# A last FFN on unnormalized tiles, a final norm on transposed tiles, and three weight borders moved by 64 bytes

## The chip, the core and the metric

The kernel runs on one core of a Trainium2 chip. The metric is the device time of one execution in microseconds (us). TensorE (PE) multiplies, VectorE (DVE), ScalarE (ACT) and GpSimd (POOL) do the work on tiles, SyncE (SP) issues every DMA. The page and the trace come from one profiled execution; "span" is the time from its first to its last instruction.

## The reference, cut to what matters

The input is one sequence of 256 tokens with 1024 features. Two hybrid attention layers run first and then a second block of two layers with shift, scale and gate vectors that depend on a condition. Each layer of the second block is a half FFN, a mixer (Fourier, then retention), and another half FFN. The diff touches the last FFN and the final norm most.

```python
def half_ffn(t, m, j):
    h = modulate(rmsnorm_2(t, norm_g[l, j]), m[3 * j], m[3 * j + 1])      # h * (1 + scale) + shift
    return t + 0.5 * m[3 * j + 2] * swiglu(h, ffn_w_gate[l, j // 2], ffn_w_up[l, j // 2], ffn_w_down[l, j // 2])
...
x = x + m_lat[5] * y_lat          # end of the retention mixer
x = half_ffn(x, m_lat, 2)         # the last FFN, on the 256 tokens of x only
return rmsnorm_2(x, final_g)
```

`rmsnorm_2` divides by the root of the mean square over the 1024 features of a token; `swiglu` is silu(h @ w_gate) * (h @ w_up), 2816 wide, times w_down.

## The kernel before, in words

**Layout.** Activations lie transposed: 128 features on the partitions, tokens along the free axis, so x is 8 tiles (`KT`) of 128 x 256 (`T`). A weight matrix arrives in chunks of 128 x 1024 float32, one output tile per chunk. Every product is made of three matmuls in float32r, on a high and a low part of both operands: `w_high` x `h_high`, `w_high` x `h_low`, `w_low` x `h_high` (lines 1861 to 1863 in `products`, 1873 to 1875 in `one`, 2357 to 2359 in `ro`). One chunk is thus 24 matmuls.

**Weight ring.** Chunks go round in a ring of 4 slots. SP loads `raw`, ACT copies it to `w_high` (`split`, line 565), POOL subtracts to get `w_low` (line 1021), three chunks ahead of TensorE (`AHEAD`). `W8` puts the split weights at an offset of 64 bytes in the slot (`LINE` = 16 floats), `WIDE` at 0. Chunks used with 256 columns mostly take the first form and chunks used with 512 columns (x and context together) the second, but the first three chunks of `up0`, `up1` and `up2` are `WIDE` although their matmuls have 256 columns each: they run twice, once for each half (`chunk_trio`), while the norm before them is still being finished.

**Order.** Each engine runs a list written out by hand, with counting semaphores between them. The stages near the end are `rg` and the retention heads, `ro` (16 chunks, two for each tile of x), a norm, `up3` (44 chunks: gate and up tiles in turns), `down3` (32 chunks, four for each tile of x), the final norm and one store.

**The norm before `up3`.** During `ro` DVE adds each output tile to x (line 1814), squares it (1173) and adds the squares (1176). After the last tile TensorE sums over the partitions with a matmul on a matrix of ones (1836), ACT takes the root (612), DVE the reciprocal (1154); then tile by tile DVE multiplies by gain and 1/root (1162), ACT adds the shift (621) and copies the high part (625), POOL makes the low part (1050). TensorE waits for tile after tile (`tile_ready`).

**`up3`.** For each pair of chunks ACT takes SiLU of the gate bank (865), DVE multiplies it with the up bank (1572) and casts the product to its high part (1575), POOL makes the low part (`act_low`, 1111). The PSUM banks of a pair are used again two pairs later.

**The end.** In `down3` DVE adds and squares each tile (1600, 1173, 1176). Then the same norm without a shift: sum, root, reciprocal, eight multiplications on DVE and eight copies on ACT (634), and one store of 1 MB (551) in feature order; the host transposes the result.

Of the kernel before, what the change touches and what calls it, by code (L numbers as in the profile page):

```python
# [164 lines left out]
def program(nc, xT_d, cols_d, cond_d, ada_d, w1_d, wv_d, wu_d, wd_d, w2_d, rope_d, mask_d, ident_d, identb_d,  # L165
            dft_d, rope2_d, dist_d, out_d):
    with ExitStack() as ctx:
# [39 lines left out]
        rs = keep("rs", [P, 2 * T])  # L207
        sT = at("sT", [P, 4, T], F32, top[0])
# [6 lines left out]
        top8 = keep("top8", [P, 8])  # L215
        late = top[0] + (x_at - top[0]) % 256
# [145 lines left out]
        own_std = sem("own_std")  # L362
        stored = sem("stored")
        passed = sem("passed")
# [73 lines left out]
        def _(e):  # L438
# [111 lines left out]
            e.wait_ge(normed, 4 + 3 * KT)  # L550
            e.dma_start(out_d.rearrange("(k p) t -> p k t", p=P), hf[:, :, 0:T]).then_inc(stored, 16)
            e.wait_ge(stored, 16)
# [3 lines left out]
        def _(e):  # L556
# [51 lines left out]

            def norm(cols_n, shift, dest, has_split):

                e.wait_ge(sq_summed, n_sq())
                e.activation(rs[:, 0:cols_n], ps[:, 7, 0:cols_n], ACT.Sqrt, bias=eps[:, :], scale=1.0 / D)\
                    .then_inc(std_done, 1)
                if has_split and shift:
                    with turns(e, KT // 4, (n_scaled, 4), (n_shifted, 4)) as i:
                        for pair in ((0, 1), (2, 3)):
                            for j in pair:
                                e.wait_ge(scaled, n_scaled())
                                for q in range(cols_n // T):
                                    part = nb[:, j, T * q:T * q + T]  # L620
                                    last = e.activation(part, part, ACT.Identity, bias=shift(4 * i + j, q))
                                last.then_inc(shifted, 1)
                            for j in pair:
                                e.wait_ge(shifted, n_shifted())
                                e.activation(flat(hh, 4 * i + j, 0, cols_n), nb[:, j, 0:cols_n], ACT.Copy)\
                                    .then_inc(norm_hi, 1)
                    return
                with turns(e, KT // 4, (n_scaled, 4)) as i:
                    for j in range(4):
                        e.wait_ge(scaled, n_scaled())  # L630
                        for q in range(cols_n // T):
                            src, out = nb[:, j, T * q:T * q + T], dest(4 * i + j, q)
                            if shift is None:
                                last = e.activation(out, src, ACT.Copy)
                            else:
                                last = e.activation(out, src, ACT.Identity, bias=shift(4 * i + j, q))
                        last.then_inc(norm_hi if has_split else normed, 1)
# [208 lines left out]
            stepped(laps("out"), W8, WIDE, 0, OUT, None, context_and_squares)  # L846
# [10 lines left out]
            def up(f, halves, all_split=None):  # L857
                base = later[f"up{f}"]

                def silu(i, j):  # L860
# [4 lines left out]
                    e.activation(tn[:, j // 2, 0:halves * T], ps[:, j - 1, 0:halves * T], ACT.Silu)\  # L865
                        .then_inc(act_step, 1)

                if f < ADA_FFNS:
                    e.wait_ge(cond_in, 16 * LAYERS + 32 * f + 32)
                    e.wait_ge(norm_split, all_split)  # L870
                    for q in range(2):
                        e.activation(cond_bank(q), ada2[q][:, :], ACT.Silu).then_inc(c_silu, 1)
# [274 lines left out]
        def _(e):  # L1147
# [674 lines left out]
            with turns(e, KT // 2, (step, 4)) as i:  # L1822
                for j in range(2):
                    add_tile(3, 5, 2 * i + j, j, 1)
# [690 lines left out]
```

## Time and profile before

| | us |
|---|---|
| runs (3) | 2327.92, 2334.66, 2335.64; median 2334.66 |
| the profiled execution, its own time | 2331.55 |
| its span | 2329.8 |
| PE busy in the span | 2269.9 |
| POOL busy | 1352.6 |
| DVE busy | 1105.4 |
| ACT busy | 843.7 |

A timeline row reads: start, duration, engine, line, operation, output and inputs, shape, count; in brackets the idle time of the engine before it and what ended it. The duration of a matmul is its passage through the pipeline, so neighbours overlap; the distance between two starts is what one costs in a stream. In the windows view PEclk is the granted TensorE clock, 1.00 for 2.4 GHz and 0.50 for 1.2 GHz.

### The profile page before, as it was taken

What the parts mean: (1) busy time and instruction counts of PE and PEld (TensorE: products, weight loads), DVE (VectorE), ACT (ScalarE), POOL (GpSimd) and SP (SyncE); (2) the same over time, 40 slices, a digit from 0 to 9 for tenths busy, and PEclk for the clock granted to TensorE, in tenths of its full rate; (3) what the DMA queues carried; (4) which work ended last, traced back from release to release, by engine and by line L of the source; (5) the groups of instructions that cost most, each with busy time, mean ns of one, the idle gap of its engine ahead of it and who ended that gap; (6) DMA issues with size and microseconds to landing.
All of it is one profiled execution on the core that took longest, in us unless ns stands there. A gap on an engine that the chain in (4) does not pass through costs nothing.

```text
span 2329.8 us, 39284 instructions
## 1 busy us (share of the span) xinstructions
PE 2269.9 (97%) x13534; PEld 1997.9 (86%) x13534; DVE 1105.4 (47%) x2078; ACT 843.7 (36%) x1250; POOL 1352.6 (58%) x712
## 2 busy tenths in 40 slices
PE   8999999999999999999999999999999999998997
PEld 7988999888888888868888888888888988998997
DVE  6753468543765543267555422655522520245223
ACT  5454453544522212213322222422222423655653
POOL 6864788647665554403555443555544544468996
PEclk9999999999999999999999999999999999998998
DMA  8842468523365543301655433455533422224554
GB/s 290 272 145 73 136 230 290 185 80 124 121 226 198 197 143 100 115 31 55 226 180 201 158 93 98 172 202 194 190 92 96 167 91 100 97 98 150 188 180 135
DMA packets 112846, 356.58 MB, mean 153 GB/s; under 512 B 13168, under 2 KB 22896, under 8 KB 112368
## 3 DMA queue, kind: packets, MB, share of 16 engines
q1 hardware_dynamic: 112752, 355.31, 46.1%
q8 instruction: 61, 1.00, 0.2%
q14 instruction: 33, 0.27, 0.0%
HBM read 347.66 MB, written 1.05 MB: 150 GB/s over the span
## 4 chain that ended last, share of the span: by engine, by line
PE 82%; POOL 6%; DVE 4%; issue 4%; ACT 1%; DMA 1%; DVEq 0%; SPq 0%; POOLq 0%; ACTq 0%
PE ps L1861 22%; PE ps L1862 22%; PE ps L1863 22%; POOL w_low L1021 5%; PE ps L1992 2%; PE ps L2010 1%; PE ps L1912 1%; PE ps L1911 1%; PE ps L1910 1%; PE ps L2223 1%; PE ps L2319 1%; PE ps L2213 1%; DMA raw<-in_w_dram 1%; PE ps L2000 1%; DVE ps L1288 1%
## 5 line engine op out<-in xcount | busy, mean ns | idle before, releaser
L1021 POOL TENSOR_TENSOR w_low<-raw,w_high 128x1024 fp32r<-128x1024 f32 (+3 forms) x542 | 1204.5, 2232 | 685.5 <-ACT w_high L565 684.7
L565 ACT ACTIVATE w_high<-raw 128x1024 fp32r<-128x1024 f32 (+3 forms) x544 | 537.6, 990 | 1142.4 <-PE ps L1863 902.1
L1861 PE MATMUL ps<-h_high,w_high 128*128 128x256 f32 (+1 forms) x2720 | 892.4, 328 | 22.5 <-POOL h_low L1050 6.4
L1862 PE MATMUL ps<-h_low,w_high 128*128 128x256 f32 (+1 forms) x2720 | 882.3, 324 | 0.0
L1863 PE MATMUL ps<-h_high,w_low 128*128 128x256 f32 (+1 forms) x2720 | 882.1, 324 | 0.0
L1861 PEld LDWEIGHTS ps<-h_high,w_high 128*128 128x128 f32 x2720 | 515.7, 190 | 70.5 <-issue 9.2
L1863 PEld LDWEIGHTS ps<-h_high,w_low 128*128 128x128 f32 x2720 | 516.3, 190 | 42.8
L1862 PEld LDWEIGHTS ps<-h_low,w_high 128*128 128x128 f32 x2720 | 515.7, 190 | 42.6
L1861 PE MATMUL ps<-act_high,w_high 128*128 128x512 f32 (+1 forms) x770 | 266.2, 346 | 0.0
L1862 PE MATMUL ps<-act_low,w_high 128*128 128x512 f32 (+1 forms) x770 | 265.6, 345 | 0.0
L1863 PE MATMUL ps<-act_high,w_low 128*128 128x512 f32 (+1 forms) x770 | 265.6, 345 | 0.0
L1572 DVE TENSOR_TENSOR hn<-tn,ps 128x512 f32<-128x512 f32 (+1 forms) x88 | 54.7, 621 | 382.9 <-PE ps L1863 318.3
L1111 POOL TENSOR_TENSOR act_low<-hn,act_high 128x512 f32 (+3 forms) x88 | 102.0, 1159 | 210.6 <-DVE act_high L1575 210.6
L1862 PEld LDWEIGHTS ps<-act_low,w_high 128*128 128x128 f32 x770 | 145.1, 188 | 18.2
L1863 PEld LDWEIGHTS ps<-act_high,w_low 128*128 128x128 f32 x770 | 145.1, 188 | 18.1
L1861 PEld LDWEIGHTS ps<-act_high,w_high 128*128 128x128 f32 x770 | 145.1, 188 | 18.0
L1247 DVE SCALAR_TENSOR_TENSOR sq<-ada,ps 128x1024 f32<-128x1024 f32 x120 | 146.5, 1221 | 17.2
L1243 DVE SCALAR_TENSOR_TENSOR sq<-ada,ps 128x1024 f32<-128x1024 f32 x120 | 146.1, 1218 | 8.9 <-DMA ada<-in_ada_dram 0.3
L1600 DVE SCALAR_TENSOR_TENSOR x<-ps,gate,x 128x256 f32 (+1 forms) x50 | 22.3, 481 | 262.6 <-PE ps L1863 262.2
L1873 PE MATMUL ps<-h_high,w_high 128*128 128x256 f32 x248 | 75.6, 305 | 14.6 <-DVE h_low L1186 8.2
L1910 PE MATMUL ps<-w_high,h_high 128*128 128x512 f32 (+1 forms) x224 | 83.6, 373 | 1.6 <-POOL w_low L1021 1.6
L1912 PE MATMUL ps<-w_high,h_low 128*128 128x512 f32 (+1 forms) x224 | 83.3, 372 | 0.0
(213 smaller groups left out, 2332.0 us busy)
## 6 DMA issues: line engine op xcount, KB each, us to landing
raw<-in_w_dram SPq DMA_DIRECT2D x216, 512.0 KB, 3.5
raw<-in_wu_dram SPq DMA_DIRECT2D x176, 512.0 KB, 4.5
ada<-in_ada_dram SPq DMA_DIRECT2D x144, 512.0 KB, 4.0
raw<-in_wd_dram SPq DMA_DIRECT2D x64, 384.0 KB, 3.1
raw<-in_wd_dram SPq DMA_DIRECT2D x64, 320.0 KB, 2.9
raw<-in_wv_dram SPq DMA_DIRECT2D x24, 408.0 KB, 4.8
heads<-rot SPq DMA_DIRECT2D x96, 64.0 KB, 3.6
ada<-in_cond_dram SPq DMA_DIRECT2D x6, 512.0 KB, 5.0
```

The lines of the kernel that those rows point to most:

```text
L565: e.activation(wh[:, c % RING, at_:at_ + w], raw[:, c % RING, 0:w], ACT.Copy).then_inc(hi_done, 1)
L1021: e.tensor_tensor(wl[:, c % RING, at_:at_ + w], raw[:, c % RING, 0:w], wh[:, c % RING, at_:at_ + w].bitcast(F32), ALU.subtract).then_inc(l ...
L1111: e.tensor_tensor(flat(al, 2 * i + j // 2, 0, halves * T), hn[:, j // 2, 0:halves * T], flat(ah, 2 * i + j // 2, 0, halves * T).bitcast(F3 ...
L1243: e.scalar_tensor_tensor(out=trash, in0=ada2[half][:, :], scalar=1.0, in1=cond_bank(0), op0=ALU.mult, op1=ALU.mult, accum_out=mod[:, bass. ...
L1247: e.scalar_tensor_tensor(out=trash, in0=ada2[half][:, :], scalar=1.0, in1=cond_bank(1), op0=ALU.mult, op1=ALU.mult, accum_out=mod[:, bass. ...
L1572: e.tensor_tensor(hn[:, j, 0:w], tn[:, j, 0:w], ps[:, 2 * j + 1, 0:w], ALU.mult)\
L1861: e.matmul(ps[:, bank, to:to + n], wh[:, j, w], hi, start=(first and t == tiles[0]), stop=False)
L1862: e.matmul(ps[:, bank, to:to + n], wh[:, j, w], low, start=False, stop=False)
L1863: end = e.matmul(ps[:, bank, to:to + n], wl[:, j, w], hi, start=False, stop=(last and t == tiles[-1]))
L1873: e.matmul(out, wh[:, j, w], hi, start=first, stop=False)
L1910: e.matmul(out, hh[:, k, tok], wh[:, j, w], start=(first and t == 0), stop=False)
L1912: end = e.matmul(out, hl[:, k, tok], wh[:, j, w], start=False, stop=(last and t == 1))
```

## The change

**Last FFN.** The high and low parts of x times gain are made tile by tile during `ro`, without the factor 1/root and without the shift. 1/root is a factor per token, that is per column of the output, so DVE multiplies both PSUM banks of each pair with it after the product. The shift is a vector over features, the same for all tokens; it is laid beside the tiles as two more columns (`T:T+2` of `h_high` and `h_low`, one for either half of the condition), so that the same matmuls, now 258 columns wide, give W x shift in column 256, and ACT (as bias of SiLU) and DVE (as scalar of the product) add it. The squares are summed during `ro` by ACT (square) and DVE (addition, in PSUM). TensorE starts `up3` with two chunks side by side (`duo`: tiles 0 to 6 of chunk 0, then of chunk 1, then tile 7 of both), and then does the sum over partitions.

**Final norm.** ACT multiplies each tile with `final_g` while `down3` runs; after it TensorE sums the squares per token with one-column matmuls and transposes the tiles to token order; root and reciprocal are on 2 columns, and DVE and ACT scale 512 columns at a time, each two times, with 1/root as a scalar per partition. Four stores of 256 KB replace one of 1 MB, and the host does not transpose.

**Borders.** The first three chunks of `up0`, `up1` and `up2` are split at 64 bytes (`W8`), and `chunk_trio` reads them there.

```diff
+        shifts = keep("up_shifts", [P, 2, 2])
+        xg = at("x_scaled", [P, KT, T], F32, tn_at)
+        fin = at("final", [P, TT, D], F32, h_at)
...  SP
-            e.dma_start(out_d.rearrange("(k p) t -> p k t", p=P), hf[:, :, 0:T]).then_inc(stored, 16)
+            for b in range(2):
+                for tt, ready in ((0, rows_by_dve), (1, rows_by_act)):
+                    part = slice(D // 2 * b, D // 2 * b + D // 2)
+                    e.wait_ge(ready, b + 1)
+                    e.dma_start(out_rows[:, tt, part], fin[:, tt, part]).then_inc(stored, 16)
...  ACT
-            stepped(laps("out"), W8, WIDE, 0, OUT, None, context_and_squares)
+            stepped(laps("out"), W8, W8, 0, OUT, None, context_and_squares)
...
-            norm(T, mod_shift(1, 6), to_hh, True)
-            up(3, 1)
+            def mixed_tile(o):
+                new = ps[:, 6 + o % 2, 0:T]
+                e.wait_ge(mixed_in, o + 1)
+                e.activation(hh[:, o, 0:T], new, ACT.Copy, scale=gain[:, 5, o:o + 1, 0]).then_inc(norm_hi, 1)
+                if o >= 2:
+                    e.wait_ge(mixed_added, o - 1)
+                e.activation(sq[:, 1, T * (o % 2):T * (o % 2) + T], new, ACT.Square).then_inc(mixed_squared, 1)
+                e.activation(xk(o, 1)[:, 0, :], new, ACT.Copy).then_inc(mixed_copied, 1)
+            stepped(later["ro"], W8, W8, 1, 2 * KT - 1, None, tile_of_pair)    # mixed_tile(k // 2 - 1) at even k
+            mixed_tile(KT - 1)
+            fourth(later["up3"], W8)
+            table_for_sqrt()
+            std(5)
+            last_up()      # per pair: wait for up_scaled, SiLU with bias=shifts[:, j // 2, 0:1]
...
+            def gained(o):     # called once per tile during down3
+                e.wait_ge(emptied_d, 4 + d0 + RING * o + RING)
+                e.activation(xg[:, o, :], xk(o, 1)[:, 0, :], ACT.Copy, scale=col("final_g_2", o)).then_inc(x_gained, 1)
...
+            for b in range(2):
+                e.wait_ge(x_turned, KT // 2 * b + KT // 2)
+                e.activation(fin[:, 1, D // 2 * b:D // 2 * b + D // 2], ps[:, 4 + b, :], ACT.Copy, scale=rs[:, 1:2])\
+                    .then_inc(rows_by_act, 1)
...  DVE, ro
+                e.scalar_tensor_tensor(out=new, in0=new, scalar=gate[:, 4, o:o + 1, 0], in1=xk(o, 1)[:, 0, :],
+                                       op0=ALU.mult, op1=ALU.add).then_inc(mixed_in, 1)
+                e.wait_ge(norm_hi, hi0 + o + 1)
+                e.wait_ge(mixed_copied, o + 1)
+                e.scalar_tensor_tensor(out=hl[:, o, 0:T], in0=new, scalar=gain[:, 5, o:o + 1, 0],
+                                       in1=hh[:, o, 0:T].bitcast(F32), op0=ALU.mult, op1=ALU.subtract)\
+                    .then_inc(norm_split, 1)
...  DVE, up3
+            with turns(e, 2 * FT // RING, (n_act, 2), (n_up, 4), (step, 2)) as i:
+                for j in range(2):
+                    gated_by, linear = ps[:, 2 * j, 0:T], ps[:, 2 * j + 1, 0:T]
+                    e.wait_ge(chunk_done, 1 + m0 + RING * i + 2 * j + 2)
+                    e.tensor_copy(shifts[:, j, :], ps[:, 2 * j:2 * j + 2, T:T + 1].rearrange("p a b -> p (a b)"))\
+                        .then_inc(up_scaled, 1)
+                    e.tensor_tensor(gated_by, gated_by, rs[:, 0:T], ALU.mult).then_inc(up_scaled, 1)
+                    e.tensor_tensor(linear, linear, rs[:, 0:T], ALU.mult).then_inc(dve_step, 1)
+                    ...
+                    e.scalar_tensor_tensor(out=hn[:, j, 0:T], in0=linear, scalar=shifts[:, j, 1:2], in1=tn[:, j, 0:T],
+                                           op0=ALU.add, op1=ALU.mult).then_inc(emptied_d, 2)
+                    e.wait_ge(emptied_d, 4 + d0 + RING * i + 2 * j + 2)
+                    e.tensor_copy(flat(ah, 2 * i + j, 0, T), hn[:, j, 0:T]).then_inc(act_hi, 1)
...  TensorE
-            norm(T, True)
-            up(3, 1)
+            duo(m0, (0, 1), 0, lambda c: None, tile_ready, T + 2)
+            e.wait_ge(sq_done, n_sq())
+            total(5, T, sq[:, 0, 0:T])
+            for j in (2, 3):
+                e.wait_ge(lo_done, RING + m0 + j + 1)
+                products(j, j, range(KT), 0, h, 0, T + 2, True, True, None, 0, LINE).then_inc(chunk_done, 1)
+            with e.Fori(0, n // RING - 1) as i:
+                for j in range(RING):
+                    e.wait_ge(lo_done, RING + m0 + RING + RING * i + j + 1)
+                    e.wait_ge(emptied_d, d0 + RING + RING * i + j - j % 2 + 2)
+                    products(j, j, range(KT), 0, h, 0, T + 2, True, True, None, 0, LINE).then_inc(chunk_done, 1)
             down_loop(3, T, KT // 2)
-            norm(T, False)
+            e.wait_ge(sq_done, n_sq())
+            token_sums(0, True)
+            for o in range(KT):
+                if o == KT - 3:
+                    e.wait_ge(last_squared, 1)
+                    token_sums(1, False).then_inc(sq_summed, 1)
+                e.wait_ge(x_gained, o + 1)
+                for tt in range(TT):
+                    lo = o % (KT // 2) * P
+                    end = e.transpose(ps[:, 2 + 2 * tt + o // (KT // 2), lo:lo + P], xg[:, o, P * tt:P * tt + P], ident[:, :])
+                end.then_inc(x_turned, 1)
...  chunk_trio
-                    end = one(c, c, k, k, T * q, T, c not in began, (k, c) == here[-1], line)
+                    end = one(c, c, k, k, T * q, T, c not in began, (k, c) == here[-1], LINE)
```

## Rows read from the trace of the kernel before

**Rows 1.** The page's first part, whole span.
```profile
PE 2269.9 (97%) x13534; PEld 1997.9 (86%) x13534; DVE 1105.4 (47%) x2078; ACT 843.7 (36%) x1250; POOL 1352.6 (58%) x712
```

**Rows 2.** Timeline of TensorE, end of `ro` and end of `down3`.
```profile
2121.02 0.28 PE L2359 MATMUL ps<-gated,w_low 128*128 128x256 f32 x1
...
2130.35 0.55 PE L1861 MATMUL ps<-h_high,w_high 128*128 128x256 f32 x1 [6.07 <-POOL h_low L1050]
...
2314.90 0.28 PE L1863 MATMUL ps<-act_high,w_low 128*128 128x256 f32 x1
```

**Rows 3.** Windows: stretch, length, busy PE, PEld, DVE, ACT, POOL, PEclk, DMA share, GB/s.
```profile
2130.30:2137.60 7.30, 6.92 (x28) 6.34 (x29) 2.84 (x4) 6.66 (x14) 5.61 (x8) 0.50 0.00 1
2140.00:2200.00 60.00, 60.00 (x532) 60.00 (x531) 16.43 (x22) 39.58 (x43) 57.42 (x33) 1.00 0.54 184
1474.30:1482.00 7.70, 7.70 (x53) 7.67 (x53) 0.00 (x0) 4.02 (x4) 0.00 (x0) 0.79 0.37 132
```

**Rows 4.** Timeline of TensorE: ends of runs of evenly spaced starts.
```profile
2149.78 0.28 PE L1861 MATMUL ps<-h_high,w_high 128*128 128x256 f32 x1
...
2151.48 0.28 PE L1861 MATMUL ps<-h_high,w_high 128*128 128x256 f32 x1
...
2104.77 0.28 PE L2359 MATMUL ps<-gated,w_low 128*128 128x256 f32 x1
...
639.23 0.28 PE L1875 MATMUL ps<-h_high,w_low 128*128 128x256 f32 x1
...
644.99 0.28 PE L1875 MATMUL ps<-h_high,w_low 128*128 128x256 f32 x1
...
645.34 0.40 PE L1862 MATMUL ps<-h_low,w_high 128*128 128x512 f32 x1
...
654.88 0.39 PE L1862 MATMUL ps<-h_low,w_high 128*128 128x512 f32 x1
...
107.00 0.35 PE L1912 MATMUL ps<-w_high,h_low 128*128 128x408 f32 x1
...
110.92 0.34 PE L1912 MATMUL ps<-w_high,h_low 128*128 128x408 f32 x1
```

**Rows 5.** Timeline of DVE, the last tile of `ro`.
```profile
2121.57 0.48 DVE L1814 SCALAR_TENSOR_TENSOR x<-ps,gate,x 128x256 f32 x1 [1.23 <-PE ps L2359]
```

**Rows 6.** Groups by line and form, whole span.
```profile
L2043 PE MATMUL ps<-ident,prob 128*128 128x128 f32 x144 | 26.6, 276 | 0.0
...
L1651 DVE COPY pq<-ps 128x512 f32<-128x512 f32 x16 | 11.0, 689 | 9.7 <-PE ps L2213 9.6
...
L949 ACT ACTIVATE vr<-ps 128x512 f32<-128x512 f32 x16 | 9.3, 598 | 13.8 <-PE ps L1912 13.8
```

**Rows 7.** Timeline of POOL in `ro` and `up3`.
```profile
2084.56 38.00 POOL L1021 TENSOR_TENSOR w_low<-raw,w_high 128x1024 fp32r<-128x1024 f32 x15
...
2177.22 0.74 POOL L1111 TENSOR_TENSOR act_low<-hn,act_high 128x256 f32 x1 [0.35 <-DVE act_high L1575]
...
2182.67 0.74 POOL L1111 TENSOR_TENSOR act_low<-hn,act_high 128x256 f32 x1
```

**Rows 8.** Timeline of all engines, the end.
```profile
2315.44 0.48 DVE L1600 SCALAR_TENSOR_TENSOR x<-ps,gate,x 128x256 f32 x1 [4.65 <-PE ps L1863]
...
2318.86 1.75 DVE L1154 RECIPROCAL rs<-rs 128x256 f32<-128x256 f32 x1 [2.02 <-ACT rs L612]
...
2324.93 0.41 SPq L551 DMA_DIRECT2D out_dram<-hf  x1
```

**Rows 9.** DMA issues of the whole span; last number, us to landing.
```profile
x<-in_xT_dram SPq DMA_DIRECT2D x4, 256.0 KB, 5.6
...
out_dram<-hf SPq DMA_DIRECT2D x1, 1024.0 KB, 4.5
...
heads<-rot SPq DMA_DIRECT2D x8, 32.0 KB, 1.8
```

**Rows 10.** Chain of work that ended last: start, us, what.
```profile
1996.87 6.91 PE ps L2319 x32
```

More of the change, by code:

```diff
@@ L207, in program @@
         rs = keep("rs", [P, 2 * T])
+        tn_at = top[0]
         sT = at("sT", [P, 4, T], F32, top[0])
@@ L607, in _ @@
             lap_of = [None]
[L609 to L637, printed above, removed]
             def to_hh(k, q):
@@ L1149, in _ @@
             n_std, n_normed, n_nsplit = Tally(), Tally(), Tally()
-            def norm(cols_n, split, gain_of):
-                e.wait_ge(std_done, n_std())
-                e.reciprocal(rs[:, 0:cols_n], rs[:, 0:cols_n]).then_inc(dve_step, 1)
-                e.wait_ge(dve_step, step())
-                e.sem_inc(passed, 1)
-                freed, n_freed = (norm_split, n_nsplit) if split else (normed, n_normed)
-                with turns(e, KT // 4, (n_freed, 4)) as i:
-                    for j in range(4):
-                        e.wait_ge(freed, n_freed())
-                        for q in range(cols_n // T):
-                            last = e.scalar_tensor_tensor(out=nb[:, j, T * q:T * q + T],
-                                                          in0=xk(4 * i + j, 2)[:, q, :], scalar=gain_of(4 * i + j, q),
-                                                          in1=rs[:, T * q:T * q + T], op0=ALU.mult, op1=ALU.mult)
-                        last.then_inc(scaled, 1)
             def no_squares(w):
@@ L1818, in _ @@
-            e.sem_inc(sq_done, 1)
-            norm(T, True, mod_gain(5))
-            up(3, 1)
-            no_squares(T)
-            with turns(e, KT // 2, (step, 4)) as i:
+            hi0 = H_SPLITS + 8 * KT
+            shift6 = mod[:, ADA + 6 * KT:ADA + 7 * KT, :]
+            e.wait_ge(chunk_done, 1 + m0)
+            e.tensor_copy(hh[:, :, T:T + 2], shift6).then_inc(dve_step, 1)
+            own(1)
+            e.tensor_tensor(hl[:, :, T:T + 2], shift6, hh[:, :, T:T + 2].bitcast(F32), ALU.subtract)\
+                .then_inc(shift_split, 1)
@@ L1823, in _ @@
+            no_squares(T)
+            with turns(e, KT // 2 - 1, (step, 4)) as i:
                 for j in range(2):
                     add_tile(3, 5, 2 * i + j, j, 1)
+            add_tile(3, 5, KT - 2, 0, 1)
             e.sem_inc(sq_done, 1)
-            norm(T, False, lambda k, q: col("final_g_2", k))
+            m0, _, _, n = later["down3"]
+            e.wait_ge(chunk_done, 1 + m0 + n)
+            xs = xk(KT - 1, 1)[:, 0, :]
+            e.scalar_tensor_tensor(out=xs, in0=ps[:, 1, 0:T], scalar=gate[:, 5, KT - 1:KT, 0], in1=xs, op0=ALU.mult,
+                                   op1=ALU.add).then_inc(emptied_d, RING)
@@ L1829, in _ @@
+            e.wait_ge(std_done, n_std())
+            e.reciprocal(rs[:, 0:TT], rs[:, 0:TT]).then_inc(root_inverse, 1)
+            e.wait_ge(root_inverse, 1)
+            for b in range(2):
+                e.wait_ge(x_turned, KT // 2 * b + KT // 2)
+                e.tensor_scalar(fin[:, 0, D // 2 * b:D // 2 * b + D // 2], ps[:, 2 + b, :], rs[:, 0:1], None, ALU.mult)\
+                    .then_inc(rows_by_dve, 1)
         @block.tensor
@@ L1831, in _ @@
             n_sq, n_split = Tally(), Tally()
-            def norm(cols_n, split):
-                e.wait_ge(sq_done, n_sq())
-                e.matmul(ps[:, 7, 0:cols_n], ones[:, :], sq[:, 0, 0:cols_n], start=True, stop=True)\
-                    .then_inc(sq_summed, 1)
-                if split:
-                    n_split(KT)
             def total(bank, cols_n, *parts):
```

138 lines of the change are left out of this document (93 added, 45 removed).

## The prediction

> **What bounds the kernel.** I read the page first: TensorE's matmuls cover 97% of the span [rows 1], so only what empties or slows TensorE can change the time. Busy time hides the pace, so I next took the stretches around the places that the diff touches. Two are weak. The timeline shows the first [rows 2]: the last matmul of `ro` starts at 2121.02, the first of `up3` at 2130.35, after 6.07 us of waiting for `h_low`, since that norm needs the last tile, the sum, the root and the reciprocal before any tile exists. For 7.3 us more the granted clock is 0.50 [rows 3], 1.2 instead of 2.4 GHz. The second is the end: after the last matmul (2314.90) come 14.9 us of final norm and store.
>
> The price of the first gap: from 2140 on the starts stand 113.3 ns apart [rows 4] (15 in 1.70 us). 1056 matmuls of `up3` and 528 of `down3` end with a start at 2314.90; 1583 steps back is 2135.5. Without a gap `up3` would have begun at 2121.14, so gap and slow clock together cost 14.4 us.
>
> **The change, part by part.**
>
> *Norm before `up3`.* Now the tiles x times gain need no sum; the sum is needed only by the outputs. The tail of the chain for tile 7: DVE's update (0.48 us, from 2121.57 [rows 5]), ACT's copy and two more activations (0.5 each at most; 512 columns take 0.60 [rows 6]), DVE's low part (0.48) and hand-overs: ready near 2124.2. TensorE meanwhile does 42 matmuls on tiles 0 to 6, until about 2126.1. Two microseconds of cover; without cover, each late microsecond of the tile is one of TensorE. Weights: POOL has the first three chunks split by 2122.6 (15 splits without a break from 2084.56 [rows 7]); chunk 3's high part follows tile 7 on ACT and its low part is ready near 2127.1, due 2130; chunk 4 waits on ACT behind the root, near 2131.8, due 2133. Chunk 5 stands on ACT behind the first SiLU, which now waits for DVE (reciprocal 1.75 us [rows 8], copy of shifts, one multiplication), and on POOL behind the first `act_low`: ready near 2136.0, due 2136.1 at my pace. I count 0 for it, 0.7 us if TensorE is quicker. The sum over partitions, formerly inside the gap, now lies on the path: 0.6 us. Gain 14.4 - 0.6 = 13.8 us. With no idle stretch the clock should not fall either; that is in the 14.4.
>
> *258 columns instead of 256.* All 1056 matmuls of `up3` now carry two columns of shift. Nothing in the trace has that width, so I compare surcharges, pace less column time at 2.4 GHz [rows 4]: 256 columns with weights at 64 bytes 6.6 ns here and, in `ro`, 11.1 (138 starts in 16.25 us, 117.8 ns); 256 with unshifted weights 13.3 (48 in 5.76 us, 120.0); 512 unshifted 13.8 (42 in 9.54 us); 408 unshifted 16.7 (21 in 3.92 us, 186.7). The only count that is no multiple of 16 pays 3.4 ns above its kind. For 258 (107.5 ns of columns) that gives 107.5 + 6.6 + 3.4 = 117.5; with the unshifted surcharge 120.8. I take the middle, 119.2: 1056 x 5.9 ns = 6.2 us lost. Bounds: 114.1 (0.8 us) and 107.5 + 16.7 = 124.2 (11.5 us).
>
> The Trainium skill (TensorE: Matmul & The Clock Gate, Back-to-back issue gap) gives column time plus 2.5 ns, so two columns would cost 0.8 ns each time, 0.9 us in all; the trace disagrees with its level, 113.3 against 109.2 for 256 and 186.7 against 172.5 for 408, and the disagreement grows at the odd width.
>
> *New work per pair in `up3`.* DVE gets a copy of two numbers and two multiplications (at the 0.48 us of [rows 5] at most 1.5 us in all). DVE is busy 16.4 of 60 us there [rows 3]; a bank pair has a whole pair's time (5.4 us) to be freed, the chain needs about 2.5. Cost 0. POOL is the one to watch: two weight splits and an `act_low` take 5.45 us (2177.22 to 2182.67 [rows 7]), 5.80 where `act_low` waits 0.35 us for DVE's cast; TensorE needs 48 x 113.3 ns = 5.44 before, 5.72 at my pace. POOL keeps up or is a hair short: 0. What POOL saves (8 `h_low` tiles) lay in the gap.
>
> *`ro`.* DVE's two square operations become one on PSUM; ACT gets three activations, 1.5 us, per tile. A tile's two chunks last 48 x 117.8 ns = 5.65 us, and either engine needs under 4 of them. Cost 0; were ACT's splits late, POOL would pass that on at once.
>
> *Final norm.* Before, from DVE's last update (2315.44) to the end at 2329.8 are 14.4 us [rows 8]. Now: update 0.48, ACT square 0.6 with hand-over, two 1-column matmul pairs 0.6, root 0.35, reciprocal of two columns 0.35, makes 2.4; the first 512-column scaling 0.69 (ACT's nearest row 0.60, DVE's 0.69 [rows 6]), then issue at +3.2. The 16 transposes (26.6 us for 144 is at most 0.19 each) run beside this chain. Storing: the 1024 KB store landed 4.5 us after its issue [rows 9] and 0.4 us of ending follows: +8.1, a gain of 6.3 us. There are four stores now, issued some 0.45 us apart, the last at +4.6; with the 1.8 us of a 32 KB one the end is +6.8 (gain 7.6), with 5.6, as the four 256 KB loads of x took, +10.6 (gain 3.8). I take 6.3, since the same bytes move.
>
> The Trainium skill (SBUF — State Buffer, Summary: rules for kernel authors) asks for one DMA and not several where the transfer bounds; that would add about three issues, some 1.3 us, and stays inside my bounds. No run here shows it yet.
>
> *Borders.* Three borders (`up0`, `up1`, `up2`) have 144 matmuls each whose weights move to 64 bytes. Only those after the last wait for a tile count, 48 or so at each (the 48 steps at 120.0 ns above are such a run): before it TensorE waits for DVE's `h_low` in any case, and what it saves goes into that wait. 144 x 6.7 ns = 1.0 us, 0.3 if they fall to the pace of `ro`; I take 0.8. One risk: at `up2` the granted clock is 0.79 over 7.7 us [rows 3], that is 3.2 us at half clock, 1.6 us lost; slightly longer waits could move such a dip in or out.
>
> Sum: 13.8 - 6.2 + 6.3 + 0.8 = 14.7 us. On the profiled execution, 2331.55 - 14.7 = 2316.9. That execution lies 3.1 us under the median of the runs shown, so against 2334.66 I forecast 2320.0.
>
> **Rivals.**
> 1. *Columns cost only their time* (114.1 ns). Gains 5.4 us more, less 0.7 for chunk 5: 2315.3. For it: 256 and 512 unshifted pay the same 13 to 14 ns. Against: 408. Chance 0.22. The Trainium skill's gap rule, named above, is this rival.
> 2. *The pace is worse*: 124.2 ns in `up3`, and `down3` entered without a stop keeps the 117.8 of `ro` (528 x 4.5 = 2.4 us). For it: `ro`, with shifted weights, never reached 113.3, and `up3` now follows it with no gap. 14.7 - 5.3 - 2.4 = 7.0: 2327.7. Chance 0.18.
> 3. *POOL becomes the bound*, `act_low` waiting for the cast at each pair: 22 x (5.80 - 5.44) = 7.9 in place of 6.2: 2321.7. Against: the 0.35 waits are gone after 2177 in the trace. Chance 0.04.
> 4. *Slower*: the two columns form a pass of their own in the array, or push the matmul to the slow form of plain float32, whose 256 columns take 216 ns for each of two records [rows 10]. Everything else gains 20.9 us, so it decides from 113.3 + 20.9/1.056 = 133 ns on; at one record's 216 the time would be 2422. Against: 408 columns run at 186.7, no second pass. Chance 0.06.
>
> That the stall merely moves (tile 7 or chunk 3 late) would show as a wait of a few us at the end of `ro`; the 2 us of cover speak against it.
>
> **Numbers.** Forecast 0.50, rivals 0.22, 0.18, 0.04, 0.06. About 0.3%, 7 us, is what a measurement of this kernel tells from no change. Faster: 0.50 + 0.22 + 0.04 and 0.02 of rival 2, 0.78; same: the other 0.16 of rival 2; slower 0.06. Range: the best bounds together give 13.8 - 0.8 + 7.6 + 1.0 = 21.6 (2313), the worst 13.8 - 11.5 + 3.8 + 0.3 - 2.4 = 4.0 (2330.7); the runs before scatter by some us too, so 2312 to 2331.
>
> **What would show it.** Starts in `up3` near 119 ns apart (114 or 124 for rivals 1 and 2); no wait over 1 us between `ro` and `down3` and a granted clock of 1.00 there; from the last matmul of `down3` to the end about 8.5 us; `up1`'s last run of border matmuls at 113 instead of 120. I am wrong if the width costs over 125 ns or less than 114, if ACT, now holding SiLU for DVE, makes splits late so that TensorE waits for `w_low` in `up3`, or if the four stores land one after the other.

## The result, and the profile after

| | before | after |
|---|---|---|
| median of 20 runs each | 2329.5 us | 2318.3 us |
| lowest, highest | 2324.4, 2337.3 | 2313.2, 2325.5 |
| profiled execution (span) | 2331.55 (2329.8) | 2319.02 (2317.2) |

The ratio of the times is 0.9946, with a 95% interval of 0.9936 to 0.9955: faster by 0.54%, some 12.6 us (the two medians of the table stand 11.2 us apart). The forecast was 14.7 us less. Its 2320.0 was counted from the 2334.66 of three runs; against the 2329.5 of all twenty, 14.7 us less is 2314.8. That 2320.0 lies so near the measured 2318.3 is in part luck.

The first thing to read is where TensorE stands at three moments: the first matmul of `up3`, the first of `down3`, the last of `down3`. The timeline of TensorE in the changed kernel has (start us, busy us, engine, line, tiles, form, count):

```profile
2121.43 0.28 PE L2412 MATMUL ps<-gated,w_low 128*128 128x256 f32 x1
...
2121.54 0.28 PE L1926 MATMUL ps<-h_high,w_high 128*128 128x258 f32 x1
...
2249.45 0.28 PE L1916 MATMUL ps<-h_high,w_low 128*128 128x258 f32 x1
2249.57 0.28 PE L1914 MATMUL ps<-act_high,w_high 128*128 128x256 f32 x1
...
2309.31 0.28 PE L1916 MATMUL ps<-act_high,w_low 128*128 128x256 f32 x1
```

The 6 us of waiting of [rows 2] are gone: `up3` starts 0.11 us behind `ro`. From the last start of `ro` to the last of `down3` it was 2314.90 - 2121.02 = 193.88 us and is 187.88: 6.0 us gained. The windows (columns as in [rows 3]) show that the clock stays up where it had stood at 0.50:

```profile
2121.40:2130.30 8.90, 8.90 (x74) 8.85 (x73) 3.16 (x4) 4.37 (x8) 4.44 (x3) 1.00 0.50 168
2130.30:2137.60 7.30, 7.30 (x63) 7.30 (x62) 3.31 (x10) 5.11 (x7) 6.46 (x4) 1.00 0.29 89
```

The waits of TensorE between 2088 and 2310 us (waited for, us in total, times, longest) have one entry, and the kernel before has no such wait:

```profile
PE ps L2410 <- DVEq L1839: 1.4, 1, 1.4
```

It stands in `ro`, ahead of tile 2, whose matmuls write the PSUM bank that tile 0 had, and it is new. That bank is given back only when DVE has made the low part, and DVE waits for ACT's copies, which stand behind a weight split. Timeline of DVE and of TensorE:

```profile
2086.04 0.49 DVE L1831 SCALAR_TENSOR_TENSOR ps<-ps,gate,x 128x256 f32<-128x256 f32 x1 [2.37 <-PE ps L2412]
2088.18 0.48 DVE L1835 SCALAR_TENSOR_TENSOR h_low<-ps,gain,h_high 128x256 fp32r<-128x256 f32 x1 [1.65 <-ACT x L1009]
...
2088.78 0.39 PE L2410 MATMUL ps<-gated,w_high 128*128 128x256 f32 x1 [1.36 <-DVEq L1839]
```

The step from one start to the next is 1.64 us there and was 0.41. The 285 starts behind it stand 113.4 ns apart where they stood 117.8, which gives the 1.2 us back. Nothing shows this pace to be a gain of the change: borders and final_norm (below), whose `ro` is that of the kernel before, also run it at 113.4, without the wait, and need 46.15 us for `ro` in place of 47.42.

The chain behind the last tile of `ro`, timeline of DVE:

```profile
2121.81 0.49 DVE L1831 SCALAR_TENSOR_TENSOR ps<-ps,gate,x 128x256 f32<-128x256 f32 x1 [2.31 <-PE ps L2412]
2123.46 0.48 DVE L1835 SCALAR_TENSOR_TENSOR h_low<-ps,gain,h_high 128x256 fp32r<-128x256 f32 x1 [1.16 <-ACT x L1009]
...
2128.45 1.76 DVE L1850 RECIPROCAL rs<-ps 128x256 f32<-128x256 f32 x1 [3.92 <-ACT ps L667]
```

The tile is complete at 2123.94 (the prediction said 2124.2), while TensorE has work until about 2126.6. The root and the reciprocal, which had stood between `ro` and `up3`, now run beside matmuls.

The end, timeline of all engines ([rows 8] before):

```profile
2309.70 0.48 DVE L1879 SCALAR_TENSOR_TENSOR x<-ps,gate,x 128x256 f32<-128x256 f32 x1 [4.44 <-PE ps L1916]
2310.22 0.42 ACT L1034 ACTIVATE sq<-x 128x256 f32<-128x256 f32 x1 [5.37 <-DVE x L1879]
...
2311.45 0.26 ACT L1037 ACTIVATE rs<-ps,eps 128x2 f32<-128x2 f32 x1 [0.42 <-PE ps L2453]
2311.75 0.17 DVE L1882 RECIPROCAL rs<-rs 128x2 f32<-128x2 f32 x1 [1.56 <-ACT rs L1037]
2311.95 1.26 ACT L1042 ACTIVATE final<-ps,rs 128x512 f32<-128x512 f32 x2 [0.23 <-PE ps L2466]
2311.95 1.41 DVE L1886 TENSOR_SCALAR final<-ps,rs 128x512 f32<-128x512 f32 x2
2312.73 1.82 SPq L571 DMA_DIRECT2D out_dram<-final  x4
```

From the last matmul to the end it was 14.87 us and is 7.9: 7.0 us gained. The reciprocal on 2 columns takes 0.17 us where that on 256 took 1.75.

What is left of the difference lies before all this. The last start of `ro` is 0.4 us *later* than before. At 595.6 us, ahead of every edit, the profiled execution of the changed kernel was already 1.8 us behind; it made up 1.1 over the borders and 0.2 between them and `ro`. So 6.0 + 7.0 - 0.4 = 12.6, the difference of the spans.

### The profile page after: what moved, and what is told of

Read it like the earlier page. It is cut to its first block, busy times and chain, and to the rows that moved or that the text cites. A ratio compares the mean times of both kernels' runs of the same rounds, so it can differ in the third digit from the quotient of the medians.

```text
span 2317.2 us, 39184 instructions
## 1 busy us (share of the span) xinstructions
PE 2271.2 (98%) x13556; PEld 1999.7 (86%) x13556; DVE 1125.4 (49%) x2129; ACT 823.0 (36%) x1244; POOL 1342.7 (58%) x704
## 4 chain that ended last, share of the span: by engine, by line
PE 83%; POOL 5%; issue 4%; DVE 4%; ACT 1%; DMA 1%; SPq 0%; DVEq 0%; POOLq 0%; ACTq 0%
PE ps L1914 22%; PE ps L1916 22%; PE ps L1915 22%; POOL w_low L1060 5%; PE ps L2045 2%; PE ps L2063 1%; PE ps L1964 1%; PE ps L1963 1%; PE ps L1965 1%; PE ps L2276 1%; PE ps L2372 1%; PE ps L2266 1%; DMA raw<-in_w_dram 1%; PE ps L2053 1%; DVE ps L1300 1%
## 5 line engine op out<-in xcount | busy, mean ns | idle before, releaser
L1914 PE MATMUL ps<-h_high,w_high 128*128 128x256 f32 (+2 forms) x2704 | 887.9, 328 | 16.1 <-DVE rot L1237 6.1
L1915 PE MATMUL ps<-h_low,w_high 128*128 128x256 f32 (+2 forms) x2704 | 878.2, 325 | 0.0
L1916 PE MATMUL ps<-h_high,w_low 128*128 128x256 f32 (+2 forms) x2704 | 878.1, 325 | 0.0
L1584 DVE TENSOR_TENSOR hn<-tn,ps 128x512 f32<-128x512 f32 x66 | 45.4, 688 | 288.0 <-PE ps L1916 258.1
L1926 PE MATMUL ps<-h_high,w_high 128*128 128x256 f32 (+1 forms) x264 | 80.3, 304 | 14.6 <-DVE h_low L1198 8.3
```

The lines of the kernel that those rows point to most:

```text
L1914: e.matmul(ps[:, bank, to:to + n], wh[:, j, w], hi, start=(first and t == tiles[0]), stop=False)
L1915: e.matmul(ps[:, bank, to:to + n], wh[:, j, w], low, start=False, stop=False)
L1916: end = e.matmul(ps[:, bank, to:to + n], wl[:, j, w], hi, start=False, stop=(last and t == tiles[-1]))
L1926: e.matmul(out, wh[:, j, w], hi, start=first, stop=False)
```

## The experiments

Twelve runs were made, ten with other kernels and two with the same two once more. The table has what each trace shows: from the first start of `up3` to the first of `down3` (1056 matmuls of weights and the two of the sum), the mean distance of the last 960 starts of `up3`, the mean distance in `down3`, and from the last start of `down3` to the end. Each ratio is to the kernel before as it ran beside that kernel (its medians there: 2329.2 us for no_columns, two_wide, borders and final_norm, 2328.7 for the last four rows).

| kernel | up3, us | ns a start | down3, ns | end, us | median, us | ratio to before (95%) |
|---|---|---|---|---|---|---|
| before | (131.6) | 113.3 | 113.3 | 14.9 | 2329.5 | |
| changed | 128.03 | 120.8 | 113.3 | 7.9 | 2318.3 | 0.9946 (0.9936 to 0.9955) |
| no_columns | 123.95 | 117.1 | 117.8 | 7.9 | 2314.5 | 0.9925 (0.9902 to 0.9948) |
| two_wide | 126.00 | 118.9 | 113.3 | 7.9 | 2314.4 | 0.9925 (0.9904 to 0.9946) |
| borders | (135.2) | 117.8 | 117.8 | 14.3 | 2328.6 | 0.9997 (0.9981 to 1.0012) |
| final_norm | (132.0) | 113.3 | 113.3 | 7.9 | 2323.9 | 0.9972 (0.9957 to 0.9988) |
| before_again | (131.1) | 113.3 | 113.3 | 14.4 | 2324.0 | one run |
| after_again | 128.03 | 120.8 | 113.3 | 7.9 | 2313.7 | one run |
| width_264 | 127.21 | 120.0 | 113.4 | 7.9 | 2315.6 | one run |
| width_272 | 130.67 | 123.3 | 117.8 | 7.9 | 2324.0 | one run |
| two_wide_264 | 126.13 | 118.9 | 113.4 | 7.9 | 2316.4 | 0.9946 (0.9931 to 0.9960) |
| one_wide_264 | 127.15 | 120.0 | 113.3 | 7.9 | 2316.1 | 0.9943 (0.9929 to 0.9956) |
| relieved | 120.12 | 113.3 | 113.5 | 7.9 | 2309.6 | 0.9918 (0.9904 to 0.9932) |
| one_store | 128.03 | 120.8 | 113.4 | 8.5 | 2317.6 | 0.9951 (0.9937 to 0.9964) |

Figures of `up3` in brackets are those of the old norm: they start at the sum's matmul and hold the wait and the slow clock behind it.

### What do the two columns cost?

**no_columns**, the changed kernel with 256 columns:

```diff
-            duo(m0, (0, 1), 0, lambda c: None, tile_ready, T + 2)
+            duo(m0, (0, 1), 0, lambda c: None, tile_ready, T)
...
-                products(j, j, range(KT), 0, h, 0, T + 2, True, True, None, 0, LINE).then_inc(chunk_done, 1)
+                products(j, j, range(KT), 0, h, 0, T, True, True, None, 0, LINE).then_inc(chunk_done, 1)
```

> The changed kernel with 256 columns in up3 instead of 258; the shift of the last FFN is left out. Theory A, the two columns alone make the pace: up3's starts fall from 120.7 to 113.3 ns, 1056 times 7.4 ns is 7.8 us less than the changed kernel, a ratio to the kernel before of 0.9946 less 0.0033, 0.991. Rival B, the pace comes from going into up3 without a stop and not from the width: 256 columns would run at the 117.8 ns seen in ro, 3.1 us less, ratio 0.993. Rival C, the columns cost only their own time of 0.8 ns: 0.9 us less, ratio 0.994.

None of the three. The first 50 or so starts of `up3` keep the 117.8 ns that this trace has in `ro`. Behind the sum's matmuls (2124.43, two late starts) they stand 113.3 ns apart, change to 117.8 on the way, and `down3` stays there. Taking the columns away gave 4.1 us in `up3` and cost 2.3 in `down3` (62.07 us in place of 59.74). The timeline of TensorE shows where. Three times the first matmul of a chunk is followed late: at 2133.05, 2143.96 and 2149.44 the next start stands 136, 148 and 123 ns behind it. After the first two of these knocks the distance is 113.3 again, after the third 117.8, for good. The last two:

```profile
2143.85 0.28 PE L1916 MATMUL ps<-h_high,w_low 128*128 128x256 f32 x1
2143.96 0.31 PE L1914 MATMUL ps<-h_high,w_high 128*128 128x256 f32 x1
2144.11 0.28 PE L1915 MATMUL ps<-h_low,w_high 128*128 128x256 f32 x1
...
2149.33 0.28 PE L1916 MATMUL ps<-h_high,w_low 128*128 128x256 f32 x1
2149.44 0.29 PE L1914 MATMUL ps<-h_high,w_high 128*128 128x256 f32 x1
2149.57 0.28 PE L1915 MATMUL ps<-h_low,w_high 128*128 128x256 f32 x1
2149.68 0.28 PE L1916 MATMUL ps<-h_high,w_low 128*128 128x256 f32 x1
2149.80 0.28 PE L1914 MATMUL ps<-h_high,w_high 128*128 128x256 f32 x1
```

Both stand 0.15 us behind the end of a weight split of POOL (2141.42 and 2146.89, plus 2.40 for one), here its timeline:

```profile
2140.72 0.74 POOL L1141 TENSOR_TENSOR act_low<-hn,act_high 128x256 f32 x1
2141.42 4.81 POOL L1060 TENSOR_TENSOR w_low<-raw,w_high 128x1024 fp32r<-128x1024 f32 x2
2146.19 0.74 POOL L1141 TENSOR_TENSOR act_low<-hn,act_high 128x256 f32 x1
2146.89 4.80 POOL L1060 TENSOR_TENSOR w_low<-raw,w_high 128x1024 fp32r<-128x1024 f32 x2
2151.64 0.74 POOL L1141 TENSOR_TENSOR act_low<-hn,act_high 128x256 f32 x1
```

POOL has no idle time in these rows and needs 5.46 us a pair of chunks; TensorE at 113.3 ns needs 5.44. That 256-column matmuls fall to 117.8 ns after such a knock is an inference from this one trace, so it was tried.

**relieved**, no_columns with `act_low` on DVE (shift still left out):

```diff
 (POOL)
-                phase(later[f"up{f}"], up, down, act_low, ((n_act, 2),))
+                phase(later[f"up{f}"], up, down, act_low if f < 3 else None, ((n_act, 2),) if f < 3 else ())
 (DVE, up3)
                     e.tensor_copy(flat(ah, 2 * i + j, 0, T), hn[:, j, 0:T]).then_inc(act_hi, 1)
+                    e.wait_ge(act_hi, n_act.now)
+                    e.tensor_tensor(flat(al, 2 * i + j, 0, T), hn[:, j, 0:T], flat(ah, 2 * i + j, 0, T).bitcast(F32),
+                                    ALU.subtract).then_inc(act_split, 1)
```

> The kernel with 256 columns in up3 (shift left out), where act_low is now worked out by DVE and not by POOL, so that POOL has 4.8 us of work for each pair of chunks in place of 5.46. Theory A, with 256 columns POOL was a hair too slow for TensorE's 5.44 us, and its lateness knocked TensorE from 113.3 to 117.8 ns: now up3 (123.95 us there) takes 120.3 and down3 59.7 in place of 62.1, a ratio of 0.990. Rival B, the knock came from elsewhere: 117.8 ns again and a ratio of 0.9925. Rival C, DVE, whose cast already takes 2.3 us while POOL works, needs as long again for act_low and becomes the bound: over 5.5 us a pair, slower than 0.9925.

The trace is as theory A has it: 113.3 ns from end to end, `up3` 120.12 us, `down3` 59.79. The windows of no_columns (first) and relieved (second) over the same stretch show who had been short; POOL's busy time is the fifth number:

```profile
2160.00:2240.00 80.00, 80.00 (x681) 80.00 (x681) 36.58 (x71) 34.83 (x43) 77.95 (x44) 1.00 0.54 178
```

```profile
2160.00:2240.00 80.00, 80.00 (x709) 80.00 (x708) 61.29 (x87) 36.24 (x44) 72.10 (x31) 1.00 0.55 184
```

Measured against this kernel, the columns cost 128.03 - 120.12 = 7.9 us, 7.5 ns a matmul. Measured against no_columns, the same columns cost 4.08 - 2.33 = 1.75 us. The wider matmuls give POOL 5.80 us a pair, TensorE is never knocked, and `down3` comes in at 113.3. In the timed runs relieved stands 0.3% under the changed kernel, and the two intervals don't touch. From no_columns the times do not tell it (0.9918 and 0.9925). That the slack of POOL made the 6.1 us rests on one trace of each kernel, and the pace can also differ where nothing was edited: no_columns ran `ro` at 117.8 ns, the changed kernel and relieved at 113.4.

A rival to the columns as the cause of 120.8 ns is POOL itself: with the wait for the cast its pair takes 5.80 us, and that is 48 x 120.8 ns. The traces rule it out. In the changed kernel every low part from the seventh chunk on is ready 1.0 to 1.8 us before the chunk's first matmul, and 0.7 us at the nearest; in no_columns the knocks come where it is 0.15 us.

**width_264 and width_272** are the changed kernel with `T + 8` and `T + 16` for `T + 2`; the added columns are not used. Each ran once.

> The changed kernel with 264 columns in up3 in place of 258, eight of them of no use, the output being the same. Theory A, a price for every width that is no multiple of 16, on top of the columns' time: 110.0 plus 13.3 is 123.3 ns, 2.6 us more than the changed kernel. Theory B, columns are taken in groups of 16 and a width pays for the group that it opens: the pace of 272 columns, 120.0 to 120.8 ns, no change from 258. Theory C, an odd width costs more the further it is from the last multiple: above 124 ns.

> The changed kernel with 272 columns in up3 in place of 258, fourteen more of no use. Theory B, columns are taken in groups of 16: 113.3 ns of columns plus the 6.7 ns of the 256-column matmuls is 120.0 ns, no slower than 258 columns (120.8), 0 to 0.9 us less than the changed kernel. Theory A, everything above 256 pays 13.3 ns: 126.6 ns, 6.2 us more. If it stands at 124.5 it has the slow form of the pace, 113.3 plus 11.1.

264 columns run at 120.0 ns, every start alike, and are *cheaper* than 258 (120.8, in a pattern of 118 to 125 ns that recurs every eight starts). `up3` is 0.8 us shorter. Theories A and C fall. Theory B gives 264 rightly, but 272 runs at 123.3, neither at its 120.0 (or 124.5 for the slow form) nor at A's 126.6, and `down3` after it runs at 117.8. No rule in columns came out of it. The Trainium skill (TensorE: Matmul & The Clock Gate, Back-to-back issue gap) would have 110.0, 112.5 and 115.8 ns for the three widths by its formula, which it gives for an isolated matmul; it says itself that in a stream the weight loads set the spacing too. The traces lie 7.5 to 10.8 ns above the formula.

**two_wide.** The shift's low part needs no tile of its own: high and low part are the two extra columns of the high tile, only the matmuls that move that tile are wide, and the sum of the two result columns is the shift.

```diff
-                e.matmul(out, wh[:, j, w], low, start=False, stop=False)
-                return e.matmul(out, wl[:, j, w], hi, start=False, stop=last)
+                e.matmul(ps[:, bank, to:to + n2], wh[:, j, w], low, start=False, stop=False)     # n2 = 256
+                return e.matmul(ps[:, bank, to:to + n3], wl[:, j, w], hh[:, k, lo:lo + n3], start=False, stop=last)   # 258
...
-                    e.tensor_copy(shifts[:, j, :], ps[:, 2 * j:2 * j + 2, T:T + 1].rearrange("p a b -> p (a b)"))\
+                    e.reduce_sum(shifts[:, j, :], ps[:, 2 * j:2 * j + 2, T:T + 2], axis=AX_X)\
```

> The changed kernel with the shift's high and low parts as the two extra columns of one tile, so that of the three matmuls of a product only the two on the high tile are 258 wide and the one on the low tile is 256. Theory A, each matmul pays for its own width: starts 120.7, 120.7 and 113.3 ns on average 118.2, 1056 times 2.5 ns is 2.6 us less than the changed kernel, ratio 0.9935. Rival B, a mixture of widths keeps the pace of the wide ones: no change, ratio 0.9946. Rival C, a change of width costs something itself: starts above 120.7 ns and a time above that of the changed kernel.

118.9 ns, 2.0 us off `up3` where A said 2.6. So far A. Two more put it to the test, 264 in place of 258 columns, with two wide and with one (`n3 = 256`, which leaves out the product of the weights' low part with the shift):

> The kernel with two of three matmuls wide, these now 264 columns in place of 258. Theory A, what was seen with all three wide holds in the mixture too (264 columns 120.0 ns, 258 columns 120.8): starts fall from a mean of 118.9 to about 118 ns, up3 and the time 0.5 to 1.0 us less than with 258, ratio 0.992. Rival B, the mean of 118.9 came from the changes of width: no difference or slower.

> As before it, but only the matmul of high weights by high tile is wide (264 columns); the product of the weights' low part with the shift is left out. Theory A, each matmul pays for its own width and POOL, at 5.46 us for a pair of chunks, keeps up with 48 starts: mean (120.0 + 2 times 113.3) / 3 is 115.6 ns, 5.55 us a pair, up3 about 2.5 us shorter than with two wide, ratio 0.991. Rival B, POOL is close enough behind to make TensorE stumble at a chunk's first matmul, and the 256-column matmuls fall to 117.8 ns: mean 118 to 119, and down3 at 117.8 (2.3 us more): no gain on two wide, ratio 0.9925 to 0.993.

Here A falls: with two wide 264 is no better than 258 (118.9), and with *one* wide the mean is 120.0 ns, that of three wide. Nor is it a late POOL: behind the first six chunks each low part is ready 0.8 us or more before it is needed, and `down3` is at 113.3, so rival B's account does not fit either. Widths of a mixture can't be priced one at a time. By the times, two_wide (0.9925) and two_wide_264 (0.9946) are not told apart from each other or from the changed kernel; by the traces both save 1.9 to 2.0 us from `up3` on and compute all that it does.

### The parts alone

**borders** is the kernel before with the `W8` and `LINE` edits only:

```diff
-            stepped(laps("out"), W8, WIDE, 0, OUT, None, context_and_squares)
+            stepped(laps("out"), W8, W8, 0, OUT, None, context_and_squares)
...  (and so after four, down1, and in POOL)
-                    end = one(c, c, k, k, T * q, T, c not in began, (k, c) == here[-1], line)
+                    end = one(c, c, k, k, T * q, T, c not in began, (k, c) == here[-1], LINE)
```

> The kernel before with the borders' edit alone. By the prediction 0.8 us (0.3 to 1.0) faster, ratio 0.9997; from the change of distance between the two traces over the three borders (0.9, -1.1 and 1.3 us) 1.1 us, ratio 0.9995. Rival: what counts at the borders is where a stretch at half clock falls, 1.6 us each: then any ratio from 0.9986 to 1.0007, and the paces at the borders say nothing of it.

The time does not tell it from nothing. The traces do a little better: between the sums of the borders `up0` to `up1`, `up1` to `up2` and `up2` to `rq`, three traces with old borders have medians of 461.50, 365.74 and 366.03 us, eleven with new ones 461.43, 365.43 and 365.95. That is 0.5 us in all. The middle one is the clear one: the old are at 365.74, 365.74 and 365.75, eight of the eleven new between 365.41 and 365.45. Two of the eleven stand at 366.8 and 366.9, the profiled execution of the changed kernel among them: a stretch at half clock has come in (granted clock 0.91 over 20 us):

```profile
1095.00:1115.00 20.00, 18.15 (x126) 16.98 (x127) 12.96 (x27) 10.48 (x18) 2.41 (x1) 0.91 0.19 64
```

In that trace the stretch of the kernel before at `up2` [rows 3] is absent. These come and go, 1.4 us each, with new borders and with old.

This kernel showed something else. In `up3` and `down3`, where it equals the kernel before, it runs at 117.8 ns where that one runs at 113.3: 1584 x 4.45 ns = 7 us lost to nothing that was edited there. In all its trace is 5.8 us longer from the first start of `ro` to the last of `down3`. The timed runs do not bear that out (at most 0.12%, 2.8 us, by the interval), so the pace of one profiled execution can't be taken for that of all runs.

At the borders themselves the pace did change with the edit: the last run of matmuls at `up1` stands at 119.7 to 119.9 ns in the three traces with old borders, at 113.3 to 113.8 in nine with new ones and at 117.8 in two.

**final_norm** is the kernel before with the new end only (`gained`, `token_sums`, transposes, four stores, as in the diff of the change):

> The kernel before with the new final norm alone. By the prediction 6.3 us faster (3.8 to 7.6), ratio 0.9973; by the changed kernel's trace 6.9 us, from DVE's last update to the end 7.5 us in place of 14.4, ratio 0.9970. Rival: the eight early gain operations of ACT in down3 delay its splits, and TensorE waits: the gain is under 5 us and down3 shows waits for the high parts.

From the last matmul to the end it takes 7.9 us, where before and before_again have 14.9 and 14.4: 6.5 to 7.0. The eight early gain activations delay nothing (`down3` at 113.3 ns). By time 6.5 us (2.8 to 10).

**one_store:**

```diff
-            for b in range(2):
-                for tt, ready in ((0, rows_by_dve), (1, rows_by_act)):
-                    ...
-                    e.dma_start(out_rows[:, tt, part], fin[:, tt, part]).then_inc(stored, 16)
+            e.wait_ge(rows_by_dve, 2)
+            e.wait_ge(rows_by_act, 2)
+            e.dma_start(out_rows, fin[:, :, :]).then_inc(stored, 16)
```

> The changed kernel with one store of 1024 KB after all four scalings in place of four of 256 KB. Theory A, the store is bound by what the queues move (1.05 MB at 380 GB/s, 2.75 us), so what counts is when its first byte starts: the last scaling ends 0.7 us after the first store's issue, and the end comes 0.5 to 0.8 us later. Rival B, by the page's rule that one store saves issues: 0.3 to 1.3 us sooner, since the last of four issues stands 1.4 us behind the first.

The page meant there is one of the Trainium skill (SBUF — State Buffer, Summary: rules for kernel authors): it asks for one DMA and not several where the transfer bounds. That one store saves issues is my reading; the Trainium skill gives no reason there. The end of one_store, timeline of all engines:

```profile
2307.46 1.41 DVE L1884 TENSOR_SCALAR final<-ps,rs 128x512 f32<-128x512 f32 x2
2308.90 0.41 SPq L569 DMA_DIRECT2D out_dram<-final  x1
```

From the last matmul (2304.82) to the end (2313.30) it is 8.48 us in place of 7.91: theory A. The issue waits for all four scalings (at 2307.46 + 1.44; the first of four stands at +0.78), and both kinds end 4.4 to 4.5 us after their first issue. One store is 0.6 us slower here, by the trace; the times (0.9951 and 0.9946) don't separate them. Here, where the pieces do not come ready at one time, the trace goes against that rule of the Trainium skill.

### The same kernels once more

> The kernel before, unchanged, profiled once more. Theory A, the pace of 256-column matmuls with weights at 64 bytes is settled anew in each execution at either 113.3 or 117.8 ns, whichever the last stall leaves: up3 and down3 can come out at 117.8 here, 1584 times 4.5 ns or 7.1 us longer than in the first profile. Rival B, the pace belongs to the program (its code and layout): 113.3 in both stages again.

> The changed kernel, unchanged, profiled once more. Theory A, the 258 columns have one pace only, so up3 shows 120.8 ns again and hands down3 on at 113.3 ns, whatever ro ran at. Rival B: down3 is as free as any other stretch and can come out at 117.8 ns, 2.4 us longer; up3's 258 columns vary too.

The paces of `ro`, `up3` and `down3` came out as in the first profiles. At the borders they did not. At `up2`, behind two late starts (298 and 220 ns in one, 295 and 226 in the other), the changed kernel runs 42 steps at 113.3 ns in its first profile and at 117.8 in its second; timeline of TensorE, first and last start of the 42 steps in each:

```profile
1476.73 0.28 PE L1926 MATMUL ps<-h_high,w_high 128*128 128x256 f32 x1
...
1481.49 0.28 PE L1926 MATMUL ps<-h_high,w_high 128*128 128x256 f32 x1
```

```profile
1471.39 0.28 PE L1926 MATMUL ps<-h_high,w_high 128*128 128x256 f32 x1
...
1476.34 0.28 PE L1926 MATMUL ps<-h_high,w_high 128*128 128x256 f32 x1
```

So one program takes either pace at one place, from one execution to the next: theory A of before_again, on a short run. For `up3` and `down3` two profiles of a kernel are too few to say. The part ahead varies too: the last start of `ro` at 2114.46 and 2121.02 in two executions of the kernel before, at 2116.12 and 2121.43 in two of the changed one. A single pair of profiles may so differ by 7 us in stages that are the same.

## Why the prediction was right, step by step

- **Gap and slow clock, 14.4 us.** Right. 193.88 us less 1584 x 113.33 ns is 14.4. Between `ro` and `up3` no stall was left, and the granted clock is 1.00 there. A smaller one did arise inside `ro` (below).
- **What stays on the path, 0.6 us.** 187.88 - 7.91 - 179.52 = 0.45: the sum's two matmuls.
- **Columns, 6.2 us lost (119.2 ns).** The term that was mis-sized: 120.8 ns, 7.9 us. I had the middle between two surcharges, that of shifted weights plus 3.4 ns (117.5) and that of unshifted ones (120.8); the second was the true one to 0.1 ns. Shown is the pace, not why. The idea behind the 3.4 ns, a price for a width that is no multiple of 16, is refuted: over their columns' time, 264 (no multiple) and 272 (a multiple) both pay 10.0 ns, and 258 pays 13.3.
- **New work in `up3`, 0.** Right for the changed kernel. That POOL is the engine to watch was right too, and it may decide more than I gave it: no_columns, where it has no slack, lies 6.1 us behind relieved by one trace each. Rival 3 had it the other way round, as a danger of the slower pace.
- **`ro`, 0.** The sum came out, 47.42 us from first to last start before and 47.39 after, but by luck. I had compared how much work ACT and DVE have per tile and not when the chain through them gives the bank back. That cost 1.2 us of waiting, and the quicker pace, which I did not forecast and which two kernels with the old `ro` have as well, gave as much back.
- **Final norm, 6.3 us.** 6.8 from DVE's update to the end. The first scaling came at +2.25 where I had 2.4, and the four stores did not queue up one behind the other.
- **Borders, 0.8 us.** 0.5 by the medians of traces, inside my 0.3 to 1.0, of which only the 0.3 of the middle border is clear of the scatter; a stretch at half clock went at `up2` and another came at `up1`, as the risk named.
- **Rivals.** Columns at their time only: no. 124.2 ns and `down3` at 117.8: no, but `down3` did come out at 117.8 in three other kernels. That a stage entered without a stop keeps the pace of the one before is seen once, in the first 50 starts of `up3` in no_columns; the two late starts of the sum's matmuls ended it. The pace of `ro` did not reach `down3`: width_272 ran `ro` at 113.4 and `down3` at 117.8. A second pass: no.

My terms with their measured sizes give 14.4 - 0.45 - 7.9 + 6.8 + 0.5 = 13.4 us; the pair of profiles shows 12.5 and the ratio 12.6 (10.5 to 14.9). What the profiles lack of 13.4 lies ahead of `up3`, where the changed kernel's was 0.4 us behind instead of 0.5 ahead. Of the misses of the terms, 2.0 us too hopeful (columns and borders) and 0.7 too cautious, a third cancels. The measurement can't tell 14.7 from 13.4.

What stays open: what decides between 113.3 and 117.8 ns. That late weight splits can do it is made likely by no_columns and relieved, but of three knocks in no_columns only the last did, and one program takes both paces at `up2`. The kernel before, before_again, final_norm and borders all wait 6.1 us for the first `h_low` of `up3`. Over the first 7.3 us of `up3` their granted clock is 0.50, 0.50, 0.50 and, in borders, 0.58; the first three go on at 113.3 ns and borders at 117.8. No run here explains that.

## What to carry to other kernels

Moving a norm's factor from the inputs of a matmul to its outputs pays where the norm leaves the bound engine idle: here 9.2 us with next to no work and 5.2 us more for the half clock behind it. Before paying for it with extra columns, price them in the kernel itself, and with the neighbours at their new pace: by the traces the same two columns cost 7.9 us or 1.75 us, depending on which of two kernels without them they are measured against. Where two engines run within 1% of each other, giving the feeder some slack is worth a try: moving 0.7 us a pair off POOL gained 6.1 us by one trace of each kernel, removing the columns alone 1.75. When a chain on a result grows, ask also when it gives the buffer back: here that cost 1.2 us in a stage where every engine had time.

## What the runs showed of the hardware

**Two paces for one instruction.** Matmuls of 256 columns with weights at 64 bytes stood 113.3 or 117.8 ns apart for hundreds in a row, at a granted clock of 1.00, and in the stretches read here changed only behind a wait, a knock of 10 to 35 ns, or another width; not each of these changed it (in `down3` of relieved a knock of 62 ns did not). In no_columns the 1300 or so matmuls behind one late start took 4.45 ns more each. One program took 113.3 in one execution and 117.8 in the next over the same 42 steps. With weights at offset 0 such matmuls stood some 120 ns apart at the borders, in all three traces that have them so.

**A wider matmul can be quicker.** 264 columns 120.0 ns, 258 columns 120.8.

**DVE waits for POOL's running operation.** In relieved, timeline of DVE:

```profile
2139.87 0.70 DVE L1869 CAST act_high<-hn 128x256 f32 x1
2140.70 2.42 DVE L1871 TENSOR_TENSOR act_low<-hn,act_high 128x256 f32 x1
2143.04 0.15 DVE L1858 COPY up_shifts<-ps 128x2 f32<-128x2 f32 x1
2143.11 0.42 DVE L1860 TENSOR_TENSOR ps<-ps,rs 128x256 f32<-128x256 f32 x1
```

An operation on 256 columns takes 0.42 us with PSUM as input, and 2.42 with both inputs in SBUF while POOL splits weights (2.4 to 2.6 each). In the changed kernel the cast has the same length, from 2141.38 to 2143.75, and ends 0.15 us behind POOL's splits (2138.85 + 4.75). The Trainium skill (SBUF — State Buffer, Summary: rules for kernel authors) says of a DVE operation with two SBUF inputs, beside a POOL operation that reads SBUF, that the second to issue is blocked until the first is done; the trace of relieved agrees. The same section of the Trainium skill says so too of a DVE operation in a 2-port perf mode. The cast ends as if blocked so, but whether it is in that mode no run here shows. In relieved it cost nothing, since DVE had the time: it was busy for 61.3 of 80 us.
